# Block transposes of queries, keys and gated head outputs on VectorE in place of TensorE, in a two-layer decoder trunk

## The reference

```python
def reference(x, ...):
    for i in range(2):                                   # layer 0: attention, layer 1: convolution
        hn = rms_norm(x, pre_norm_g[i])
        y = moba_mixer(hn, attn_w_in, attn_w_out) if i == 0 else conformer_mixer(hn, ...)
        x = x + rms_norm(y, post_norm_g[i])

def moba_mixer(hn, w_in, w_out):                         # w_in 2048 x 8192, w_out 2048 x 2048
    q, k, v, z = jnp.split(hn @ w_in, 4, axis=-1)        # 16 heads of 128 columns
    q, k, v = apply_rope(heads(q)), apply_rope(heads(k)), heads(v)
    o = causal_softmax(q @ k.T * 128 ** -0.5) @ v        # one block of 256 rows: plain causal attention
    return (o * jax.nn.silu(z)) @ w_out
```

## Time and profile before

| | |
|---|---|
| time, median of 3 runs | 864.7 us (863.1 to 865.91) |
| the profiled execution's own time | 864.29 us |
| its span in the profile | 862.3 us |
| granted clock of TensorE over the span | 0.998 |
| busy: PE, DVE, ACT, POOL | 851.4, 573.7, 434.7, 332.8 us |

### The profile page before, as it was taken

How to read it: one execution, slowest core, us unless ns; L and a number is a source line. 1 busy time by engine, 2 the same in 40 slices (tenths; PEclk the granted TensorE clock), 3 DMA queues, 4 the chain that set the end, 5 groups by cost and what they waited for, 6 DMA issues and landing times.

```text
span 862.3 us, 12161 instructions
## 1 busy us (share of the span) xinstructions
PE 851.4 (99%) x4005; PEld 707.7 (82%) x4005; DVE 573.7 (67%) x951; ACT 434.7 (50%) x608; POOL 332.8 (39%) x169
## 2 busy tenths in 40 slices
PE   8999999999999999999999999999999999999996
PEld 6888888888888888888888888888888888888884
DVE  5656555564556455564555827999999999766555
ACT  6745354554445354454445575444454554474441
POOL 0342004400342004400000098888888879873000
PEclk9999999999999999999999999999999999999999
DMA  9965656645665656645655546555556556557532
GB/s 322 296 195 149 194 150 193 192 149 149 192 195 152 189 154 193 188 149 206 200 190 196 180 147 196 195 172 184 181 194 193 173 171 195 194 184 257 195 98 97
DMA packets 97782, 159.50 MB, mean 185 GB/s; under 512 B 3317, under 2 KB 38741, under 8 KB 97365
## 3 DMA queue, kind: packets, MB, share of 16 engines
q1 hardware_dynamic: 97156, 158.77, 57.7%
q10 hardware_dynamic: 592, 0.28, 0.1%
HBM read 156.94 MB, written 2.10 MB: 184 GB/s over the span
## 4 chain that ended last, share of the span: by engine, by line
PE 97%; issue 1%; DMA 1%; ACT 1%; DVE 0%; ACTq 0%; DVEq 0%; POOLq 0%; POOL 0%
PE acc L413 29%; PE acc L415 29%; PE acc L414 29%; PE X L423 3%; PE acc L399 1%; PE acc L401 1%; PE acc L400 1%; PE acc L481 1%; PE X L547 1%; PE acc L496 1%; DMA xrow<-in_x 1%; PE X L556 0%; PE X L541 0%; PE X L540 0%; PE X L557 0%
## 5 line engine op out<-in xcount | busy, mean ns | idle before, releaser
L785 ACT ACTIVATE w_hi<-raw 128x1024 fp32r<-128x1024 f32 x282 | 298.8, 1061 | 371.4 <-PE acc L415 371.4
L1082 DVE TENSOR_TENSOR w_lo<-raw,w_hi 128x1024 fp32r<-128x1024 f32 x182 | 242.3, 1333 | 223.8 <-ACT w_hi L785 223.4
L413 PE MATMUL acc<-w_hi,xT_hi 128*128 128x512 f32 x864 | 340.9, 395 | 0.3 <-DVE xT_lo L1101 0.3
L415 PE MATMUL acc<-w_hi,xT_lo 128*128 128x512 f32 x864 | 336.8, 390 | 0.0
L414 PE MATMUL acc<-w_lo,xT_hi 128*128 128x512 f32 x864 | 336.2, 389 | 0.0
L1485 POOL TENSOR_TENSOR w_lo<-raw,w_hi 128x1024 fp32r<-128x1024 f32 x100 | 243.2, 2440 | 49.0 <-ACT w_hi L785 48.9
L415 PEld LDWEIGHTS acc<-w_hi,xT_lo 128*128 128x128 f32 x864 | 162.2, 188 | 34.2
L413 PEld LDWEIGHTS acc<-w_hi,xT_hi 128*128 128x128 f32 x864 | 162.3, 188 | 32.7 <-DVE xT_lo L1101 0.5
L414 PEld LDWEIGHTS acc<-w_lo,xT_hi 128*128 128x128 f32 x864 | 162.4, 188 | 32.2
L1311 DVE SCALAR_TENSOR_TENSOR X<-u_pad,taps,X 128x256 f32<-128x256 f32 x464 | 182.7, 483 | 0.2
L1449 POOL TENSOR_TENSOR small<-small 128x1 f32<-128x1 f32 (+1 forms) x7 | 4.3, 617 | 233.7 <-DVE small L1257 126.9
(11 more groups left out here) (155 smaller groups left out, 704.6 us busy)
## 6 DMA issues: line engine op xcount, KB each, us to landing
raw<-in_w_in SPq DMA_DIRECT2D x78, 1024.0 KB, 5.3
raw<-in_w_in SPq DMA_DIRECT2D x66, 512.0 KB, 4.5
raw<-in_w_out SPq DMA_DIRECT2D x32, 1024.0 KB, 5.1
gpost<-in_post_g SPq DMA_DIRECT2D x2, 1024.0 KB, 4.8
raw<-in_w_in SPq DMA_DIRECT2D x4, 256.0 KB, 4.8
xrow<-in_x SPq DMA_DIRECT2D x2, 512.0 KB, 9.6
bout<-in_b_out SPq DMA_DIRECT2D x1, 1024.0 KB, 7.0
out<-xrow SPq DMA_DIRECT2D x4, 256.0 KB, 2.8
```

The source lines that it names most:

```text
L413: nc.tensor.matmul(a, hi[:, k, rows], w_hi[:, slot, i], start=(k == 0), stop=False)
L415: last = nc.tensor.matmul(a, lo[:, k, rows], w_hi[:, slot, i], start=False, stop=(k == KT - 1))
L785: nc.scalar.activation(w_hi[:, slot], raw[:, u % LOADS, 2 * half:2 * half + 2], ACT.Copy).then_inc(hi_ready[slot], 1)
L1082: nc.vector.tensor_tensor(lo_of(first, it, s), raw[:, u % LOADS, 2 * half:2 * half + 2], hi_of(first, it, s).bitcast(f32), ALU.subtract).t ...
```

## The change

- PE's transposes of queries, keys and gated outputs are gone (`pair_T` stays for the second layer), and with them ACT's copies to `qT` and `kT`.
- `turn`: DVE transposes the rotated queries behind `low(15)` and `low(16)`, the rotated keys behind `low(23)` and `low(24)`. One instruction turns the 32x32 blocks between 32 source partitions and 32 destination partitions, for four heads and both halves of the rows: 256 elements in a partition. 16 instructions make `qT` or `kT`.
- `heads_turned`: the gated outputs are transposed into the new tile `uT` in SBUF in two calls of two heads, behind `low(4)` and `low(5)`, 16 instructions of 128 elements each. `gate_outputs` stands behind `low(3)` in place of `low(4)`. `uT_hi` is made from `uT` by ACT in two parts behind `high(7)` and `high(8)`, `uT_lo` by DVE in two parts behind `low(6)`.
- PE waits for `qT_ready` and `kT_ready` behind slice 22, and in the output projection for one half group of `uT_lo` per slice.
- POOL waits for its own last query step ahead of the key rotation.

```diff
+BLK = 32
+        uT = at("uT", C + 27 * KB, [P, G, SEQ])
...
-            def gated_T(g):
-                pe.wait_ge(u_ready, g + 1)
-                pair_T(u_row, X[2], 0)
-                pair_T(u_row, X[3], 2).then_inc(uT_done, 1)
...
-                    if s == 3 and not first:
-                        gated_T(g - 1)
...
-                    if s == 14:
-                        pe.wait_ge(rope_step, 6 * g + 3)
+                    if s == 22:
                         if first:
                             pe.wait_ge(vec_ready, 2)
                         else:
                             pe.wait_ge(u_ready, g)
-                        pair_T(q_row, X[0], 0)
-                        pair_T(q_row, X[1], 2).then_inc(qT_done, 1)
-                    if s == 20:
-                        pe.wait_ge(rope_step, 6 * g + 6)
-                        if not first:
-                            pe.wait_ge(ulo_ready, g)
-                        pair_T(k_row, X[2], 0)
-                        pair_T(k_row, X[3], 2).then_inc(kT_done, 1)
-                    if s == 22:
                         pe.wait_ge(qT_ready, g + 1)
                         pe.wait_ge(kT_ready, g + 1)
...
-                if s % 2 == 0 and s < SLICES:
-                    pe.wait_ge(ulo_ready, s // 2 + 1)
+                if s < SLICES:
+                    pe.wait_ge(ulo_ready, s + 1)
...
-            def heads_high(g):
-                act.wait_ge(uT_done, g + 1)
-                for b in range(2):
-                    last = nc.scalar.activation(uT_hi[:, bass.ds(g * 4 + 2 * b, 2)], X[2 + b][:], ACT.Copy)
-                last.then_inc(uhi_ready, 1)
+            def heads_high(g, i):
+                act.wait_ge(uT_ready, 2 * g + i + 1)
+                nc.scalar.activation(uT_hi[:, bass.ds(g * 4 + 2 * i, 2)], uT[:, 2 * i:2 * i + 2], ACT.Copy
+                                     ).then_inc(uhi_ready, 1)
...
-                if s == 7:
-                    heads_high(g)
+                if s in (7, 8):
+                    heads_high(g, s - 7)
...
-                    if s == 18:
-                        act.wait_ge(qT_done, g + 1)
-                        for b in range(2):
-                            last = nc.scalar.activation(qT[:, 2 * b:2 * b + 2], X[b][:], ACT.Copy)
-                        last.then_inc(qT_ready, 1)
...
-                    if s == 24:
-                        act.wait_ge(kT_done, g + 1)
-                        for b in range(2):
-                            last = nc.scalar.activation(kT[:, 2 * b:2 * b + 2], X[2 + b][:], ACT.Copy)
-                        last.then_inc(kT_ready, 1)
...
+            def heads_turned(g, i):
+
+                dve.wait_ge(u_ready, g + 1)
+                if not (isinstance(g, int) and g == 0):
+                    dve.wait_ge(ulo_ready, 2 * g)
+                heads = slice(2 * i, 2 * i + 2)
+                for a in range(4):
+                    for b in range(4):
+                        last = nc.vector.transpose(
+                            uT[b * BLK:(b + 1) * BLK, heads].rearrange("p h (m c) -> p m h c", m=MT)
+                            [:, :, :, a * BLK:(a + 1) * BLK],
+                            u_row[a * BLK:(a + 1) * BLK].rearrange("p m (h c) -> p m h c", h=G)
+                            [:, :, heads, b * BLK:(b + 1) * BLK])
+                last.then_inc(uT_ready, 1)
...
             def group_end(s, g):
-                if s == 4:
+                if s == 3:
                     gate_outputs(g)
-                if s == 7:
-                    heads_low(g)
+                if s in (4, 5):
+                    heads_turned(g, s - 4)
+                if s == 6:
+                    heads_low(g, 0)
+                    heads_low(g, 1)
+
+            def turn(dst, row, quadrants, done):
+
+                for a in quadrants:
+                    for b in range(4):
+                        last = nc.vector.transpose(
+                            dst[b * BLK:(b + 1) * BLK].rearrange("p h (m c) -> p m h c", m=MT)
+                            [:, :, :, a * BLK:(a + 1) * BLK],
+                            row[a * BLK:(a + 1) * BLK].rearrange("p m (h c) -> p m h c", h=G)
+                            [:, :, :, b * BLK:(b + 1) * BLK])
+                if a == 3:
+                    last.then_inc(done, 1)
...
+                    if s in (15, 16):
+                        if s == 15:
+                            dve.wait_ge(rope_step, 6 * g + 3)
+                            if not first:
+                                dve.wait_ge(s_done, G * g)
+                        turn(qT, q_row, (0, 1) if s == 15 else (2, 3), qT_ready)
+                    if s in (23, 24):
+                        if s == 23:
+                            dve.wait_ge(rope_step, 6 * g + 6)
+                        turn(kT, k_row, (0, 1) if s == 23 else (2, 3), kT_ready)
...
             with pool.Fori(0, NG) as g:
                 rotate(q_row, 4 * g + 1, 6 * g)
+                pool.wait_ge(rope_step, 6 * g + 3)
                 rotate(k_row, 4 * g + 2, 6 * g + 3)
```

More of the change, by code:

```diff
@@ L200, in build @@
         rope_step = sem("rope_step")
-        qT_done, kT_done = sem("qT_done"), sem("kT_done")
         qT_ready, kT_ready = sem("qT_ready"), sem("kT_ready")
@@ L211, in build @@
         u_ready = sem("u_ready")
-        uT_done = sem("uT_done")
+        uT_ready = sem("uT_ready")
         uhi_ready, ulo_ready = sem("uhi_ready"), sem("ulo_ready")
@@ L614, in _ @@
                     acc_free(16 + s // SLICES)
-                if s % 2 == 0 and s < SLICES:
-                    pe.wait_ge(ulo_ready, s // 2 + 1)
+                if s < SLICES:
+                    pe.wait_ge(ulo_ready, s + 1)
                 if s < 4 * SLICES - RING:
                     slice_products(S_OUT0, 0, 0, s, uT_hi, uT_lo)
-                if s == 3:
-                    gated_T(NG - 1)
             last_slices = range(4 * SLICES - RING, 4 * SLICES)
@@ L628, in _ @@
                 if s == last_slices[-1]:
-                    pe.wait_ge(ulo_ready, NG)
+                    pe.wait_ge(ulo_ready, 2 * NG)
                     row_T(0, 0)
@@ L1152, in gate_outputs @@
                 dve.wait_ge(inv_ready, g + 1)
+                if not (isinstance(g, int) and g == 0):
+                    dve.wait_ge(uT_ready, 2 * g)
                 for m in range(MT):
@@ L1169, in group_end, with heads_low @@
+            def heads_low(g, i):
+                dve.wait_ge(uhi_ready, 2 * g + i + 1)
+                t = bass.ds(g * 4 + 2 * i, 2)
+                nc.vector.tensor_tensor(uT_lo[:, t], uT[:, 2 * i:2 * i + 2], uT_hi[:, t].bitcast(f32), ALU.subtract
+                                        ).then_inc(ulo_ready, 1)
             def group_end(s, g):
-                if s == 4:
+                if s == 3:
                     gate_outputs(g)
-                if s == 7:
-                    heads_low(g)
+                if s in (4, 5):
[3 more added lines that the diff above has]
+                    heads_low(g, 1)
```

## The result

The change made the kernel 5.1% slower: 908.9 us against 864.4 us (medians of 4 runs each), ratio 1.0506, 95% interval 1.0487 to 1.0526. The prediction had 882 us and a range up to 892: the right sign, and less than half of the loss. The profiled execution took 905.28 us, its span is 903.3 us.

A forecast was written before the change was run, and what follows sets the result against it. The prediction took PE's queue to bound the kernel. Stalls of 4 x (3.7 keys + 3.3 gated outputs) + 0.6, less 10.7 of removed transposes, gave +17.9 us on 864.3: 882 us, range 863 to 892.

The forecast's parts named there:

- What goes from PE: PE's transposes in the attention groups: twelve sets of eight at 0.89 us go, 10.7 us, the whole possible gain.
- Price of a block transpose: On DVE: 0.43 us (256 elements), 0.30 (128), no overlap, because partitions change and filling a block uses up the overlap.
- Gated outputs: Seam between groups: PE waits 3.3 us before slice 6, in each of four; 0.6 us more in the output projection.
- Keys: Scores behind slice 22: DVE's kT comes 3.7 us late for PE in each of four groups.
- Queries: DVE's turns behind low(15) and low(16): ready before PE wants slice 17, hidden with 0.47 us to spare.
- rival 4: Eight new stalls drop TensorE to 1.2 GHz for one slice each: 22 us more, 904 us; chance 0.05.
- the likeliest case: The forecast case: key and gated output stalls less PE's removed transposes, +17.9 us, 882 us; chance 0.60.
- Signs of being wrong: Transpose step not the full duration, low(23) not ending 1.08 us after POOL, or PE's clock leaving 1.00.
- Rivals 1 to 3: DVE's block transposes overlap (863 or 871 us, chance 0.18), are cheaper (853.6, 0.10), or run at half rate (931, 0.07).
- a fixed part of 0.195 us: Upper variant of a DVE transpose's fixed time, in place of 0.165 us; said to give 889 us.

The follow-up runs named there:

- The wide form: The whole change with one transpose instruction on 128 partitions in place of each four on 32, blocks left in wrong places: 852.2 us, ratio 0.9862.
- e9: e8 with ACT copying the key block out ahead of high(19) in place of behind it: 854.8 us, ratio 0.9887.
- e8: The whole change with queries in threes, gated outputs in fours, keys behind low(22) and low(23), scores behind slice 23, last group's outputs on PE: 858.8 us, ratio 0.9935.

## Why the prediction was wrong, point by point

The forecast for the profiled execution was +17.9 us and it measured +41.0. Two steps of the prediction account for the difference: the sum left out the low clock behind its own stalls (16.7 us, the larger), and it took the query part for hidden (6.1 us more of waits). 0.3 us stay open.

- **What goes from PE, 10.7 us: right.** The wide form gave it back in full, e9 the 9.8 us of its eleven sets.
- **Price of a block transpose: right.** Chosen 0.43 and 0.30 us without overlap; measured 0.436 and 0.302 us, steps of 0.45 and 0.316. The reason given had two halves. That it is the change of partitions is shown by the experiment with blocks on their own partitions. That filling a block would use up the overlap is refuted by it: the blocks were filled there too and did overlap.
- **Gated outputs, 3.3 us at slice 6 and 0.6 more at the end: right.** Measured 3.2 three times and 3.8.
- **Keys, 3.7 us: right by itself, wrong in the whole.** With keys only it was 3.7 us. In the change it was 5.4, since the path began with "POOL ends them at 70.09", taken from the trace before as if the change could not move it. POOL ended them 2.4 us later behind slice 15. `low(23)` no longer stood behind POOL, which gave back 1.05 us, and the transposes took 0.3 us more than in the sum.
- **Queries, "Hidden, with 0.47 us to spare": this step failed, for 6.1 us.** It asked only whether PE gets its low parts in time (it does) and noted that DVE's lag is gone by `low(20)`. It didn't ask what DVE does while it makes up the lag: two-input reads from SBUF without a pause, at the moment when POOL starts on the keys. This held POOL back by 2.4 us in each group. By itself the query part costs four waits of 2.2 us, 8.6 us in all. In the whole it made the waits 34.7 us in place of the forecast 28.6.
- **The clock, left out of the sum and given a chance of 0.05 as rival 4: this step failed too, for 16.7 us.** Rival 4 was priced at 22 us on top of the stalls and measured at some 16 to 18. The prediction gave no reason for its low chance. The stalls of 3 to 4 us that the forecast itself had put there were enough, as keys only shows (3.7 us each, clock 0.982). So it belonged in the sum of the likeliest case. With it that case would have been 899 us, and with POOL's delay 905, the profiled execution's 905.28. The other three executions took 908.5 to 911.1 us at a granted clock of 0.969 or 0.970 in place of 0.973; they have no trace.
- **Signs of being wrong.** Two of the three that it named came: `low(23)` did not end 1.08 us after POOL, and the clock left 1.00.
- Rivals 1 to 3 (overlap, a cheaper transpose, half rate) did not occur. A slip without weight: with a fixed part of 0.195 us the prediction's own terms give 888 us, not 889.

## What to carry to other kernels

When a kernel is bound by TensorE and is never idle, price a new stall twice: once as the wait, and once as the low clock of the work behind it. Here that was about half as much again in the change (16.7 us on 34.7), and eight tenths with the keys alone (11.8 on 14.8).

When work moves to an engine with free time on average, ask for each piece whether it fits between two of that engine's regular duties. Sixteen instructions a group in two lumps cost four waits of 2.2 us, though no deadline of its own was missed; three at a time, POOL had its pace back (a median of 744 ns), because no run of catching up came behind. One low part more beside POOL's keys was enough for 0.85 us in e8.

A time taken from the trace before is a constant only if nothing on its path can be held up by what the change adds or moves. Here POOL's end moved by 2.4 us with none of its instructions changed.

## What the runs showed of the hardware

- VectorE and GpSimd take turns when a VectorE instruction has two SBUF inputs, instruction by instruction, and both lose. In the trace before, a low part that started at 60.85 took 1.69 us in place of 1.23, and the GpSimd instruction behind its start 1.71 in place of 0.74. So each low part that meets GpSimd costs it about 1 us. Beside a run without a pause nearly every GpSimd instruction pays this: 1.71, 1.72 and 1.72 us, one behind the other. The Trainium skill, "SBUF — State Buffer", section "Who interferes with whom", has such an instruction of VectorE contend with one of GpSimd that reads SBUF, over ports that the two share under an exclusive lock; the rows agree.
- Block transposes of one SBUF input don't take part, as far as one meeting shows: in the kernel with the queries in pieces three of them ran beside GpSimd's first two key instructions, and took 1.34 us together while these took 736 and 741 ns.
- 32x32 block transposes of float32 on VectorE cost about the same on 32 partitions as on 128. The means are 0.404 us for 256 elements in a partition and 0.270 for 128 on 32 partitions, with a change of partitions at every fourth, and 0.412 and 0.278 on all 128. With a change at each one they are 0.436 and 0.302.
- TensorE's granted clock fell to 0.50 at all four stalls of 5.1 to 5.4 us and, with keys only, at all four of up to 3.7 us. At the four of 3.2 to 3.8 us before slice 6 it fell three times in the change and four times with the gated outputs only. With queries only it fell at three of four stalls of 2.2 us, and with the blocks on their own partitions at all four of up to 2.7 us. With the queries in pieces it fell at all eight stalls, of 3.2 to 4.0 us. At the three of 0.7 us in e8 it did not.
